# The last four gathers split into halves and the last norm rearranged, in a one-core streaming encoder step with expert retrieval

## The chip, the core and the metric

The kernel runs on one core of one Trainium2 chip. The metric is the device time of one execution in microseconds (us). The core has five engines that run their own instruction streams and wait for each other through semaphores: TensorE (PE, with its weight loads shown as PEld), VectorE (DVE), ScalarE (ACT), GpSimd (POOL) and SyncE (SP), and 16 DMA engines that serve the transfers issued by SP and POOL.

## What is computed

One inference step of a one-layer encoder for 384 tokens (256 of a new stream, 128 of running streams), in three tiles of 128 tokens. After attention and retention, each token goes through a layer that picks experts from a table of 16,384, and the result is normed. Only this last part is touched by the change:

```python
def rmsnorm(x, g):
    xf = x * lax.rsqrt(jnp.mean(x * x, axis=-1, keepdims=True) + EPS)
    return xf * g

def peer(h, ...):                       # 8 heads, 16 picks each: 128 picks a token
    ...                                 # e_idx: chosen experts, gate: softmax of their scores
    u = exp_u[e_idx]                    # (T, 8, 16, 1024)
    act = gelu(einsum('thkd,td->thk', u, h))
    return einsum('thk,thkd->td', gate * act, exp_v[e_idx])

x = x + peer(rmsnorm(x, ln2_g), ...)
y = rmsnorm(x, ln_final_g)
```

## The kernel before, in words

The expert tables U and V lie side by side in one HBM tensor `uv`: row `n` has the 1024 numbers of U and then the 1024 of V, 8 KB in fp32. The picks are worked off in 384 steps, n = 0 to 383: three tiles of tokens (t), eight heads in each, 16 picks a head. A head is a unit u (24 in all). A gather of step n fetches one row of 8 KB for each of the 128 partitions, 1 MB in all, into `row[n % 8]`, a ring of G = 8 buffers. A tile of 128 tokens is held twice over as two halves of 64, so an even n and the odd one after it form a pair: the even one serves 64 tokens with two picks and so does the odd one.

Each step has four stages.

- POOL (`gather`, L499) issues the gather of n once TensorE has done with the buffer: it waits for `acc`, which counts finished pairs. The gather's arrival raises `landed[s]`.
- DVE (L1879) waits for `landed[s]` and forms the dot product of the U half of the row with the token's normed vector.
- ACT (`weigh`, L1139) applies gelu, multiplies by the gate, and spreads the result into a diagonal matrix `diag[:, s, :]`: three instructions. The third raises `diagd`.
- PE (`add_experts`, L532) waits for both diagonals of the pair and multiplies them with the V halves, adding into two PSUM banks (e = 0 and e = 1, columns 0 to 511 and 512 to 1023 of the output). In the profile these are 8 records a pair. It then raises `acc`.

The order of everything that runs between these steps is written out by hand as generators, which a small clock advances once a step. In the last twenty-odd steps nothing else is left: the last unit's picks are spread in step 358 (`spread_take`, which fills `ids` and `gates`), and from there all engines only run the four stages.

Behind step 383 stands the last norm, of tile 2, in a straight line. ACT squares the two PSUM banks in one instruction of 128x1024 with a running sum (`square`), DVE turns the sum into a mean (`mean_square`, L1461), POOL raises it to the power -0.5 (`take_rstd`, L463), DVE multiplies PSUM by this factor and by the norm's weights `gfb` in two instructions of 128x512 (L1886), and SP stores each half as it is ready (L453). The program ends when both stores have landed.

```python
            mean_square(Y_STAT[2])
            dve.wait_ge(rsd, Y_STAT[2] + 1)
            dve.wait_ge(acc, UNITS * KP // 2)
            for e in range(2):
                then(V.scalar_tensor_tensor(x[:, 2, e * 512:(e + 1) * 512], ps[:, e, :], rstd[...], gfb[...], ALU.mult, ALU.mult), y_out)
```

`then` raises a semaphore with an instruction and makes DVE wait for it before the next.

Of the kernel before, what the change touches and what calls it, by code (L numbers as in the profile page):

```python
# [18 lines left out]
U32 = mybir.dt.uint32  # L19
ALU = mybir.AluOpType  # L20
# [3 lines left out]
P = 128  # L24
D = 1024
# [13 lines left out]
G = 8  # L39
# [43 lines left out]
def build(nc, a, o):  # L83
    with ExitStack() as ctx:
        def sb(name, shape, dt=F32):
            return ctx.enter_context(nc.sbuf_tensor(name, shape, dt))
# [16 lines left out]
        zdot = sb("zdot", [P, G])  # L103
        zact = sb("zact", [P, G])
        wgt = sb("wgt", [P, G])

        sumsq, ms, rstd = sb("sumsq", [P, 9]), sb("ms", [P, 9]), sb("rstd", [P, 9])
        bn6, mv = sb("bn6", [P, HB, 6]), sb("mv", [P, HB, 2])
# [165 lines left out]
        kv_out, sp_out, ss_out, y_done = sem("kv_out"), sem("sp_out"), sem("ss_out"), sem("y_done")  # L274
        sqd, msd, rsd, hready, x1_done = (sem(n) for n in ("squares", "mean_square", "rstd", "h_ready", "x1_done"))
        gained = sem("x_gained")
        ht_ps, ht_act, ht_dve = sem("ht_ps"), sem("ht_act"), sem("ht_dve")
        kv_ps, kv_sb, qi_ps, qi_sb, qa_ps, qa_sb = (sem(n) for n in ("kv_ps", "kv_sb", "qi_ps", "qi_sb", "qa_ps", "qa_sb"))
        vb_ps, vb_sb, qk_ps, rotated, gb_ps, gb_sb = (sem(n) for n in ("vb_ps", "vb_sb", "qk_ps", "rotated", "gb_ps", "gb_sb"))
# [81 lines left out]
        def _(sp):  # L361
# [87 lines left out]
            sp.wait_ge(y_out, 2)  # L449
            sp.dma_start(o["y"][1], x[:, 1, :]).then_inc(y_done, 16)  # L450
            for e in range(2):
                sp.wait_ge(y_out, 3 + e)
                sp.dma_start(o["y"][2][:, e * 512:(e + 1) * 512], x[:, 2, e * 512:(e + 1) * 512]).then_inc(y_done, 16)  # L453
            sp.wait_ge(sp_out, 16)
            sp.wait_ge(ss_out, 16)
# [2 lines left out]
        @block.gpsimd  # L458
        def _(pool):
            def take_rstd(n):  # L460

                pool.wait_ge(msd, n + 1)
                pool.tensor_tensor(rstd[:, n:n + 1], ms[:, n:n + 1], half4[:, 0:1], ALU.pow).then_inc(rsd, 1)  # L463

            def group_rstd(t):
                pool.wait_ge(o_var, t + 1)
                pool.tensor_tensor(rstd4[:], veps[:], half4[:], ALU.pow).then_inc(o_rstd, 1)

            pool.memset(euler[:], float(np.e))
            pool.memset(half4[:], -0.5).then_inc(half_set, 1)  # L470
            pool.wait_ge(half_set, 1)
            for n in range(TILES):
                take_rstd(n)
            pool.wait_ge(kv_ps, TILES)
            pool.memset(wz, 0.0).then_inc(wz_zero, 1)
            group_rstd(0)
            pool.wait_ge(wout, 2)
            pool.memset(wz, 0.0).then_inc(wz_zero, 1)
            take_rstd(H2_STAT[0])

            def gate_exp(u):

                pool.wait_ge(best_set, u + 1)
                pool.tensor_tensor(ebest[:, u % 2, :], euler[:, 0:1].broadcast_to([P, KP]), below[:], ALU.pow).then_inc(gexp, 1)  # L484

            gate_exp(0)
            gates_after = {gate_after(u): u for u in range(1, UNITS)}

            def gather(n):
                s = n % G  # L490
                if n % KP == 0:
                    pool.wait_ge(picked, n // KP + 1)
                if n == 4:
                    pool.wait_ge(qi_ps, 3)
                if n == 6:
                    pool.wait_ge(q_ps, 2)
                if n >= G:
                    pool.wait_ge(acc, (n - G) // 2 + 1)
                pool.indirect_dma_start(row[s], None, a["uv"], bass.IndirectOffsetOnAxis(  # L499
                    ap=ids[:, own(n // KP).start + n % KP:own(n // KP).start + n % KP + 1], axis=0)).then_inc(landed[s], 16)  # L500

            for n in range(UNITS * KP):
                gather(n)
                if n in gates_after:
                    gate_exp(gates_after[n])
                if n == 48:
                    group_rstd(1)
                if n == 50:
                    pool.wait_ge(o_ps, 2)
                    pool.memset(wz, 0.0).then_inc(wz_zero, 1)  # L510
                if n == 81:
                    take_rstd(H2_STAT[1])
                if n == 104:
                    pool.wait_ge(dots, CACHE + STREAMS)
                    pool.memset(qz, 0.0).then_inc(qz_zero, 1)
                if n == 124:
                    group_rstd(2)
                if n == 140:
                    take_rstd(Y_STAT[0])
                if n == 142:  # L520
                    pool.wait_ge(ss_ps, 1)
                    pool.memset(qzb, 0.0).then_inc(qzb_zero, 1)
                if n == 223:
                    take_rstd(H2_STAT[2])
                if n == 268:
                    take_rstd(Y_STAT[1])
            take_rstd(Y_STAT[2])

        @block.tensor
        def _(pe):  # L530
# [261 lines left out]
            def add_experts(n, stop=False):  # L792
                pe.wait_ge(diagd, n + 2)
                for e in range(2):
                    for j in range(2):
                        s = (n + j) % G
                        last = mm(ps[64 * j:64 * j + 64, Y_BANK[n // (HP * KP)] + e, :], diag[:, s, :], row[s][:, D + e * 512:D + (e + 1) * 512], False, stop)
                last.then_inc(acc, 1)

            mm(ps[:, 2, 0:P], e8[64:64 + HI, :], kiw[64:64 + HI, P:2 * P]).then_inc(w_ps, 1)  # L800
            index_queries(1, 6, 0, 1)
# [335 lines left out]
        def _(act):  # L1137
# [294 lines left out]
            for n in range(UNITS * KP):  # L1432
                t = n // (HP * KP)
                if n > 5:
                    weigh(n)
                if n == t * HP * KP + 1 and t > 0:
                    y_take(t - 1)
                clock.tick(n, *gens)
                if n == t * HP * KP + 3 and t > 0:
                    y_square(t - 1)  # L1440
            act.wait_ge(acc, UNITS * KP // 2)
            square(Y_STAT[2], psf[:, 0:D], h2r[0][:, 0, :])

        @block.vector
        def _(dve):
# [181 lines left out]
            def spread_take(u):  # L1627

                dve.wait_ge(spread_ps, u + 1)
                for q in range(2):  # L1630
                    r = slice(64 * q, 64 * q + 64)
                    src = spread_psum(u)[r, :].rearrange("p (j e c q) -> p e q c j", j=2, e=2, q=2)
                    V.tensor_copy(ids[r, own(u)].rearrange("p (c j) -> p c j", j=2), src[:, 0, q, :, :])
                    ins = V.tensor_copy(gates[r, own(u)].rearrange("p (c j) -> p c j", j=2), src[:, 1, q, :, :])
                then(ins, picked)

            def top16(u):
                yield from top16_halves(u)
# [233 lines left out]
            for n in range(UNITS * KP):  # L1872
# [6 lines left out]
                V.tensor_tensor_reduce(row[s][:, 0:D], row[s][:, 0:D], h2r[t % 2][:, n % 2, :], 1.0, 0.0, ALU.mult, ALU.add,  # L1879
                                       zdot[:, s:s + 1]).then_inc(dotted, 1)  # L1880
                clock.tick(n, *gens)
            mean_square(Y_STAT[2])
            dve.wait_ge(rsd, Y_STAT[2] + 1)
            dve.wait_ge(acc, UNITS * KP // 2)
            for e in range(2):
                then(V.scalar_tensor_tensor(x[:, 2, e * 512:(e + 1) * 512], ps[:, e, :], rstd[:, Y_STAT[2]:Y_STAT[2] + 1],  # L1886
                                            gfb[:, e * 512:(e + 1) * 512], ALU.mult, ALU.mult), y_out)


# ---- launch: inputs laid out for the program, outputs laid out as the reference has them  # L1890
# [56 lines left out]
```

## Time and profile before

| | |
|---|---|
| median of 3 runs | 1169.07 us (1169.01, 1169.07, 1171.17) |
| profiled execution, own time | 1169.1 us |
| its span, first to last instruction | 1167.3 us |
| mean granted TensorE clock | 0.892 of full speed |
| busy share of the span: PE, DVE, POOL, ACT | 74%, 70%, 46%, 38% |
| DMA | 461.82 MB, 396 GB/s over the span; 402.68 MB of it are the 384 gathers |

The span is 1.8 us shorter than the execution's own time; what lies around it is outside the instructions. A busy share is an average over the whole run, so the table says little about the end of the program, where the change lies. The page's row of DMA shows the 16 engines at 90% or more of their time in nearly every one of the 40 slices.

### The profile page before, as it was taken

The numbers are of one execution on the slowest core, as the hardware profiler recorded it, in microseconds if no ns is written. First come the engines' busy times: TensorE is split into PE (matmuls) and PEld (weight loads), VectorE is DVE, ScalarE is ACT, GpSimd is POOL, SyncE is SP. The second block draws the span as 40 slices with busy tenths as digits, with TensorE's granted clock in tenths as the row PEclk, the third lists the DMA queues.
The fourth block names the chain that finished last, engine by engine and source line by source line (L and its number), as shares of the span: only waits on it lengthen the run. The fifth ranks groups of instructions, "written<-read, shape, count | busy, mean of one in ns | idle before, by whom it ended". The sixth has DMA issues, their size and how long they took to land.

```text
span 1167.3 us, 12080 instructions
## 1 busy us (share of the span) xinstructions
PE 859.7 (74%) x3701; PEld 390.8 (33%) x3706; DVE 813.9 (70%) x2115; ACT 440.8 (38%) x1400; POOL 539.7 (46%) x431
## 2 busy tenths in 40 slices
PE   8999988998888757765767768577666656656554
PEld 6748644443323314322223333133222212211110
DVE  2426877875787789986877886547877777777453
ACT  2122444333444334433456553233333333333332
POOL 0002445552666455463644553445564555456441
PEclk9999999999999879787889999797989888886868
DMA  9903999999999999999999999999999999999994
GB/s 378 393 1 92 422 425 426 426 425 428 402 423 426 425 427 424 378 407 423 428 426 424 426 426 427 424 427 428 418 389 419 426 427 426 428 426 425 424 427 202
DMA packets 67057, 461.82 MB, mean 396 GB/s; under 512 B 8368, under 2 KB 10160, under 8 KB 15024
## 3 DMA queue, kind: packets, MB, share of 16 engines
q0 software_dynamic: 55296, 402.68, 82.5%
q1 hardware_dynamic: 11696, 58.37, 12.3%
q8 instruction: 29, 0.48, 0.1%
q14 instruction: 36, 0.29, 0.1%
HBM read 456.73 MB, written 3.24 MB: 394 GB/s over the span
## 4 chain that ended last, share of the span: by engine, by line
DMA 43%; PE 28%; DVE 15%; issue 6%; POOL 4%; ACT 3%; SPq 0%; DVEq 0%; POOLq 0%
DMA rows<-in_uv,ids 41%; PE ps L532 27%; DVE rows L1879 7%; POOL rows L499 4%; ACT work L1139 1%; DMA rows<-in_w_qi 1%; ACT wgt L1139 1%; DMA wt<-in_w_q 1%; POOL work L484 1%; ACT zact L1139 1%; DVE top L1476 1%; PE ps L535 1%; DVE wt L1480 1%; DVE work L1609 0%; DVE work L1613 0%
## 5 line engine op out<-in xcount | busy, mean ns | idle before, releaser
L499 POOL DMA_INDIRECT rows<-in_uv,ids x384 | 445.4, 1160 | 495.1 <-PE ps L532 428.1
L532 PE MATMUL ps<-rows,work 128*64 128x512 f32 x1536 | 458.8, 727 | 289.8 <-ACT work L1139 289.2
L1879 DVE CUSTOM_DVE_ANT_0 rows<-rows,masks 128x1024 f32<-128x1024 f32 x256 | 313.6, 1226 | 158.9 <-DMA rows<-in_uv,ids 153.0
L1139 ACT ACTIVATE zact<-zdot 128x1 f32<-128x1 f32 x384 | 77.6, 202 | 575.7 <-DVE zdot L1879 563.7
L532 PEld LDWEIGHTS ps<-rows,work 128*64 128x64 f32 x1536 | 106.4, 155 | 549.2 <-ACT work L1139 389.6
L1879 DVE CUSTOM_DVE_ANT_0 rows<-rows,wt 128x1024 f32<-128x1024 f32 x128 | 156.9, 1226 | 85.9 <-DMA rows<-in_uv,ids 80.7
L532 PE MATMUL ps<-wt 128*128 128x128 f32 (+7 forms) x599 | 155.7, 414 | 0.9 <-DVE wt L1655 0.9
L1139 ACT ACTIVATE work<-pair,wgt 128x64 f32<-128x64 f32 x384 | 133.5, 348 | 12.5
L1139 ACT ACTIVATE wgt<-zact,gates 128x1 f32<-128x1 f32 x384 | 113.1, 294 | 12.5
L532 PEld LDWEIGHTS ps<-work,wt 128*128 128x128 f32 (+1 forms) x712 | 90.1, 201 | 60.5 <-issue 60.5
L532 PEld LDWEIGHTS ps<-wt 128*128 128x128 f32 (+2 forms) x604 | 89.2, 192 | 55.3 <-issue 47.1
L532 PE MATMUL ps<-work,wt 128*128 128x128 f32 (+1 forms) x712 | 103.9, 294 | 4.8 <-DMA wt<-in_w_q 4.8
L484 POOL TENSOR_TENSOR work<-euler,below 128x16 f32<-128x16 f32 x24 | 77.9, 3245 | 21.8 <-DVE below L1593 20.4
L1139 ACT ACTIVATE wt<-ps 128x512 f32<-128x512 f32 (+5 forms) x61 | 34.7, 577 | 58.0 <-PE ps L532 44.7
L1139 ACT ACT_TABLE_LOAD x25 | 32.1, 1283 | 1.2 <-PEq L1930 0.7
L1879 DVE DVE_READ_ACCUMULATOR2_ANT zdot<- 128x1 f32 x384 | 31.5, 82 | 0.0
L532 PE MATMUL ps<-wt,work 128*128 128x512 f32 x64 | 29.3, 600 | 0.0
L1139 ACT ACTIVATE work<-ps 128x256 f32<-128x256 f32 (+2 forms) x49 | 16.8, 345 | 29.2 <-PE ps L535 14.8
L463 POOL TENSOR_TENSOR rstd<-ms,half 128x1 f32<-128x1 f32 x9 | 6.8, 760 | 38.3 <-DVE ms L1461 38.2
L532 PE MATMUL ps<-wt,rows 128*128 128x128 f32 x192 | 22.9, 276 | 1.0 <-DMA rows<-in_w_qi 1.0
L532 PEld LDWEIGHTS ps<-wt,rows 128*128 128x128 f32 x192 | 22.1, 192 | 1.7 <-DMA rows<-in_w_qi 1.5
L532 PEld LDWEIGHTS ps<-keysT,work 128*128 128x128 f32 x96 | 14.1, 210 | 24.2 <-issue 24.1
(145 smaller groups left out, 639.0 us busy)
## 6 DMA issues: line engine op xcount, KB each, us to landing
wt<-in_w_q SPq DMA_DIRECT2D x9, 2048.0 KB, 15.9
rows<-in_uv,ids POOLq DMA_INDIRECT x384
rows<-in_w_out SPq DMA_DIRECT2D x2, 2048.0 KB, 32.0
wt<-in_w_out SPq DMA_DIRECT2D x2, 2048.0 KB, 11.3
wt<-in_ckv SPq DMA_DIRECT2D x16, 256.0 KB, 14.0
x<-in_x SPq DMA_DIRECT2D x5, 512.0 KB, 8.5
rows<-in_w_qi SPq DMA_DIRECT2D x1, 2048.0 KB, 12.8
wt<-in_w_qa SPq DMA_DIRECT2D x1, 2048.0 KB, 11.6
```

The source lines that it names most:

```text
L463: pool.tensor_tensor(rstd[:, n:n + 1], ms[:, n:n + 1], half4[:, 0:1], ALU.pow).then_inc(rsd, 1)
L484: pool.tensor_tensor(ebest[:, u % 2, :], euler[:, 0:1].broadcast_to([P, KP]), below[:], ALU.pow).then_inc(gexp, 1)
L499: pool.indirect_dma_start(row[s], None, a["uv"], bass.IndirectOffsetOnAxis(ap=ids[:, own(n // KP).start + n % KP:own(n // KP).start + n % ...
L532: return nc.tensor.matmul(out, lhsT, rhs, start=start, stop=stop)
L535: return nc.tensor.transpose(out, in_, ident[0:k, 0:k])
L1139: return nc.scalar.activation(*args, **kw)
L1476: then(V.max(out=top8[:], in_=score))
L1480: then(V.match_replace(out=score, in_to_replace=top8[:], in_values=score, imm_value=TAKEN))
L1879: V.tensor_tensor_reduce(row[s][:, 0:D], row[s][:, 0:D], h2r[t % 2][:, n % 2, :], 1.0, 0.0, ALU.mult, ALU.add, zdot[:, s:s + 1]).then_inc( ...
```

## The change

The last four steps, 380 to 383, no longer fetch whole rows. `gather_last` first issues the four U halves (each 128 x 4 KB, into the same buffers, each raising `landed[s]` as before), then the V halves of 380, 381 and 382 (each with a semaphore of its own, `v_landed[0..2]`), and at last the V half of 383 as two quarters (128 x 2 KB, `v_landed[3]` and `v_landed[4]`). The row numbers for this are made from `ids` by two shifts on DVE behind the last `spread_take`, which raise `last_set`. TensorE waits for the V halves in `add_experts`, and raises `y_half` after the e = 0 matmuls of the last pair. Behind pair 378/379 it gets 9 more matmuls of 128x512 in bf16, and behind pair 380/381 two, whose results nobody reads.

The last norm is divided by column halves: ACT squares bank 0 at `y_half` and bank 1 at `acc`; DVE multiplies each bank by `gfb` into `x` ahead of the factor; the sum of both halves and EPS is one DVE instruction (the division by 1024 went into the squares' scale). When the factor is there, DVE scales columns 0 to 511 and ACT columns 512 to 1023. SP stores the first half on `y_out` and the second on `y_last`.

```diff
+            def gather_last():
+                first = UNITS * KP - 4
+                pool.wait_ge(last_set, 1)
...
+                for j in range(4):
+                    pool.wait_ge(acc, (first + j - G) // 2 + 1)
+                    s = (first + j) % G
+                    pool.indirect_dma_start(row[s][:, 0:D], None, halves, half[j]).then_inc(landed[s], 16)
+                for j in range(3):
+                    s = (first + j) % G
+                    pool.indirect_dma_start(row[s][:, D:2 * D], None, halves, half[j], element_offset=D).then_inc(v_landed[j], 16)
+                for e in range(2):
+                    s = (first + 3) % G
+                    pool.indirect_dma_start(row[s][:, D + e * 512:D + (e + 1) * 512], None, quarters, quarter,
+                                            element_offset=D + e * 512).then_inc(v_landed[3 + e], 16)
...
             def add_experts(n, stop=False):
                 pe.wait_ge(diagd, n + 2)
                 for e in range(2):
+                    if n == UNITS * KP - 4 and e == 0:
+                        pe.wait_ge(v_landed[0], 16)
+                        pe.wait_ge(v_landed[1], 16)
+                    if n == UNITS * KP - 2:
+                        if e == 0:
+                            pe.wait_ge(v_landed[2], 16)
+                        else:
+                            last.then_inc(y_half, 1)
+                        pe.wait_ge(v_landed[3 + e], 16)
...
                 last.then_inc(acc, 1)
+                if n in (UNITS * KP - 6, UNITS * KP - 4):
+                    for i in range(9 if n == UNITS * KP - 6 else 2):
+                        mm(ps[:, 6, :], ident_bf[:], ident_bf[:].rearrange("p (g t) -> p g t", g=1).broadcast_to([P, 4, P]))
...
+            act.wait_ge(y_half, 1)
+            A(h2r[0][:, 1, 0:512], ps[:, 0, :], ACT.Square, scale=D ** -0.5, accum_out=sumsq[:, 0:1]).then_inc(half_sqd, 1)
             act.wait_ge(acc, UNITS * KP // 2)
-            square(Y_STAT[2], psf[:, 0:D], h2r[0][:, 0, :])
+            A(h2r[0][:, 1, 512:D], ps[:, 1, :], ACT.Square, scale=D ** -0.5,
+              accum_out=sumsq[:, Y_STAT[2]:Y_STAT[2] + 1]).then_inc(sqd, 1)
+            act.wait_ge(rsd, Y_STAT[2] + 1)
+            act.wait_ge(gained, 4)
+            A(x[:, 2, 512:D], x[:, 2, 512:D], ACT.Copy, scale=rstd[:, Y_STAT[2]:Y_STAT[2] + 1]).then_inc(y_last, 1)
...
+                if u == UNITS - 1:
+                    four = ids[:, own(u).start + KP - 4:own(u).start + KP]
+                    V.tensor_scalar(last_ids[:, 0:4], four, 1, None, ALU.logical_shift_left)
+                    then(V.tensor_scalar(last_ids[:, 4:5], four[:, 3:4], 2, None, ALU.logical_shift_left), last_set)
...
-            mean_square(Y_STAT[2])
+            dve.wait_ge(half_sqd, 1)
+            then(V.tensor_tensor(x[:, 2, 0:512], ps[:, 0, :], gfb[:, 0:512], ALU.mult), gained)
+            dve.wait_ge(sqd, Y_STAT[2] + 1)
+            then(V.tensor_scalar(ms[:, Y_STAT[2]:Y_STAT[2] + 1], sumsq[:, 0:1], sumsq[:, Y_STAT[2]:Y_STAT[2] + 1], EPS,
+                                 ALU.add, ALU.add), msd)
+            then(V.tensor_tensor(x[:, 2, 512:D], ps[:, 1, :], gfb[:, 512:D], ALU.mult), gained)
             dve.wait_ge(rsd, Y_STAT[2] + 1)
-            dve.wait_ge(acc, UNITS * KP // 2)
-            for e in range(2):
-                then(V.scalar_tensor_tensor(x[:, 2, e * 512:(e + 1) * 512], ps[:, e, :], rstd[:, Y_STAT[2]:Y_STAT[2] + 1],
-                                            gfb[:, e * 512:(e + 1) * 512], ALU.mult, ALU.mult), y_out)
+            then(V.tensor_scalar(x[:, 2, 0:512], x[:, 2, 0:512], rstd[:, Y_STAT[2]:Y_STAT[2] + 1], None, ALU.mult), y_out)
```

What this does to the order of instructions shows at three places. The first is the end of GpSimd's row: before the change, the last unit's 16 gathers and the power (L463).

```order
L499 DMA rows<-in_uv,ids 128x2048 [waits acc] x15
L499 DMA rows<-in_uv,ids 128x2048 [waits acc,picked]
L499 DMA rows<-in_uv,ids 128x2048 [waits acc] x15
L463 TENSOR_TENSOR rstd<-ms,half 128x1 [waits mean_square]
L84 UNCONDITIONAL_BRANCH
```


After the change the last unit has 12 whole gathers, and the last four steps have nine pieces.

```order
L506 DMA rows<-in_uv,ids 128x2048 [waits acc,picked]
L506 DMA rows<-in_uv,ids 128x2048 [waits acc] x11
L520 DMA rows<-in_uv,last_ids 128x1024 [waits acc,last_set]
L520 DMA rows<-in_uv,last_ids 128x1024 [waits acc] x3
L523 DMA rows<-in_uv,last_ids 128x1024 x3
L526 DMA rows<-in_uv,last_ids 128x512 x2
L470 TENSOR_TENSOR rstd<-ms,half 128x1 [waits mean_square]
```


Four issues became nine, and the power (now L470) stands behind all of them.

The second place is the end of TensorE's row. Before the change the last two pairs read like all the others (`rows` are the gathered rows, `work` the diagonals):

```order
L532 MATMUL ps<-rows,work 64x512 [waits diagd]
L532 MATMUL ps<-rows,work 64x512 x3
L532 MATMUL ps<-rows,work 64x512 [waits diagd]
L532 MATMUL ps<-rows,work 64x512 x3
L84 UNCONDITIONAL_BRANCH
```


After the change, from pair 378/379 on:

```order
L562 MATMUL ps<-rows,work 64x512 [waits diagd]
L562 MATMUL ps<-rows,work 64x512 x3
L562 MATMUL ps<-ident_bf 128x512 x9
L562 MATMUL ps<-rows,work 64x512 [waits v_landed1,v_landed0,diagd]
L562 MATMUL ps<-rows,work 64x512 x3
L562 MATMUL ps<-ident_bf 128x512 x2
L562 MATMUL ps<-rows,work 64x512 [waits v_landed3,v_landed2,diagd]
L562 MATMUL ps<-rows,work 64x512
L562 MATMUL ps<-rows,work 64x512 [waits v_landed4]
L562 MATMUL ps<-rows,work 64x512
```


The added bf16 matmuls stand ahead of the waits for the V halves, and the last pair is cut in two by the wait for `v_landed4`.

The third place is the end of VectorE's row. Before the change (`keep` holds the norm's weights):

```order
L1879 ISA rows,zdot<-rows,masks 128x1024 [waits landed7]
L1879 ISA zdot 128x1
L1461 TENSOR_SCALAR ms<-sumsq 128x1 [waits squares]
L1886 SCALAR_TENSOR_TENSOR x<-ps,rstd,keep 128x512 [waits acc,rstd,mean_square]
L1886 SCALAR_TENSOR_TENSOR x<-ps,rstd,keep 128x512 [waits y_out]
L84 UNCONDITIONAL_BRANCH [waits y_out]
```


After the change:

```order
L1931 ISA rows,zdot<-rows,masks 128x1024 [waits landed7]
L1931 ISA zdot 128x1
L1935 TENSOR_TENSOR x<-ps,keep 128x512 [waits half_sqd]
L1937 TENSOR_SCALAR ms<-sumsq 128x1 [waits squares,x_gained]
L1939 TENSOR_TENSOR x<-ps,keep 128x512 [waits mean_square]
L1941 TENSOR_SCALAR x<-x,rstd 128x512 [waits rstd,x_gained]
L84 UNCONDITIONAL_BRANCH [waits y_out]
```


The two multiplications by the weights moved ahead of the wait for `rstd`, and one multiplication by `rstd` stays behind it; the other is ACT's.

## Rows read from the trace of the kernel before

**Rows 1.** The page of the profile: span, chain by engine, one costly group

```profile
span 1167.3 us, 12080 instructions
...
DMA 43%; PE 28%; DVE 15%; issue 6%; POOL 4%; ACT 3%; SPq 0%; DVEq 0%; POOLq 0%
...
L499 POOL DMA_INDIRECT rows<-in_uv,ids x384 | 445.4, 1160 | 495.1 <-PE ps L532 428.1
...
L1879 DVE DVE_READ_ACCUMULATOR2_ANT zdot<- 128x1 f32 x384 | 31.5, 82 | 0.0
```

**Rows 2.** Timeline of all engines from 1145 us: start, duration, engine, operation, idle before

```profile
1145.60 1.23 DVE L1879 CUSTOM_DVE_ANT_0 rows<-rows,masks 128x1024 f32<-128x1024 f32 x1 [1.25 <-DMA rows<-in_uv,ids]
...
1152.93 1.23 DVE L1879 CUSTOM_DVE_ANT_0 rows<-rows,masks 128x1024 f32<-128x1024 f32 x1 [1.22 <-DMA rows<-in_uv,ids]
...
1155.38 1.23 DVE L1879 CUSTOM_DVE_ANT_0 rows<-rows,masks 128x1024 f32<-128x1024 f32 x1 [1.21 <-DMA rows<-in_uv,ids]
...
1157.61 1.94 PE L532 MATMUL ps<-rows,work 128*64 128x512 f32 x8 [1.49 <-ACT work L1139]
...
1159.60 1.02 ACT L1139 ACTIVATE masks<-ps 128x1024 f32<-128x1024 f32 x1 [2.04 <-PE ps L532]
...
1160.74 0.15 DVE L1461 TENSOR_SCALAR ms<-sumsq 128x1 f32<-128x1 f32 x1 [4.13 <-ACT masks L1139]
1160.98 0.57 POOL L463 TENSOR_TENSOR rstd<-ms,half 128x1 f32<-128x1 f32 x1 [18.25 <-DVE ms L1461]
1161.66 1.54 DVE L1886 SCALAR_TENSOR_TENSOR x<-ps,rstd,keep 128x512 f32<-128x512 f32 x2 [0.76 <-POOL rstd L463]
1162.44 1.12 SPq L453 DMA_DIRECT2D out_y<-x  x2
```

**Rows 3.** Stretches: length, busy us of PE, PEld, DVE, ACT, POOL, PEclk, DMA share, GB/s

```profile
1105.00:1145.00 40.00, 22.26 (x62) 5.16 (x64) 19.73 (x32) 13.54 (x49) 19.52 (x16) 0.72 1.01 425
1151.00:1155.00 4.00, 2.29 (x6) 0.68 (x8) 1.95 (x4) 1.58 (x6) 0.00 (x0) 0.75 0.07 29
1163.20:1164.90 1.70, 0.00 (x0) 0.00 (x0) 0.00 (x0) 0.00 (x0) 0.00 (x0) 0.52 0.82 308
```

**Rows 4.** Timeline of GpSimd, the first and last of its last four gathers

```profile
1136.73 1.10 POOL L499 DMA_INDIRECT rows<-in_uv,ids  x1 [2.57 <-PE ps L532]
...
1141.49 1.24 POOL L499 DMA_INDIRECT rows<-in_uv,ids  x1 [0.30 <-issue]
```

**Rows 5.** DMA queues from 540 to 600 us: packets, MB, share of 16 engines

```profile
q0 software_dynamic: 3307, 24.09, 95.2%
q1 hardware_dynamic: 537, 1.44, 6.0%
```

**Rows 6.** Timeline of TensorE, four bursts: start, duration, idle before

```profile
1118.45 3.68 PE L532 MATMUL ps<-rows,work 128*64 128x512 f32 x8 [1.17 <-ACT work L1139]
...
1142.92 3.55 PE L532 MATMUL ps<-rows,work 128*64 128x512 f32 x8 [2.96 <-ACT work L1139]
1147.83 1.94 PE L532 MATMUL ps<-rows,work 128*64 128x512 f32 x8 [1.37 <-ACT work L1139]
1152.71 3.41 PE L532 MATMUL ps<-rows,work 128*64 128x512 f32 x8 [2.94 <-ACT work L1139]
```

**Rows 7.** Stretches, TensorE alone: length, PE busy, PEclk, DMA share, GB/s

```profile
6.00:8.00 2.00, 2.00 (x10) 1.00 1.05 429
1147.20:1152.60 5.40, 1.94 (x8) 1.00 0.63 267
```

**Rows 8.** Groups of instructions by line and shape: count, busy us, mean ns

```profile
L1699 DVE TENSOR_TENSOR work<-x,keep 128x512 f32<-128x512 f32 x2 | 1.4, 693 | 0.1
...
L1604 DVE TENSOR_SCALAR work<-work 128x16 uint32<-128x16 uint32 x24 | 4.3, 179 | 0.2
...
L1703 DVE TENSOR_SCALAR work<-work,rstd 128x1024 f32<-128x1024 f32 x1 | 0.8, 753 | 0.7 <-POOL rstd L463 0.7
...
L1139 ACT ACTIVATE wt<-ps 128x512 f32<-128x512 f32 x36 | 21.0, 590 | 36.7 <-PE ps L532 24.9 <-PE ps L535 11.8
```

More of the change, by code:

```diff
@@ L105, in build @@
         wgt = sb("wgt", [P, G])
+        last_ids = sb("last_ids", [P, 5], U32)
         sumsq, ms, rstd = sb("sumsq", [P, 9]), sb("ms", [P, 9]), sb("rstd", [P, 9])
@@ L276, in build @@
         gained = sem("x_gained")
+        v_landed = [sem(f"v_landed{i}") for i in range(5)]
+        last_set = sem("last_set")
+        y_half, y_last, half_sqd = sem("y_half"), sem("y_last"), sem("half_sqd")
         ht_ps, ht_act, ht_dve = sem("ht_ps"), sem("ht_act"), sem("ht_dve")
@@ L451, in _ @@
             for e in range(2):
-                sp.wait_ge(y_out, 3 + e)
+                if e == 0:
+                    sp.wait_ge(y_out, 3)
+                else:
+                    sp.wait_ge(y_last, 1)
                 sp.dma_start(o["y"][2][:, e * 512:(e + 1) * 512], x[:, 2, e * 512:(e + 1) * 512]).then_inc(y_done, 16)
@@ L500, in gather @@
                     ap=ids[:, own(n // KP).start + n % KP:own(n // KP).start + n % KP + 1], axis=0)).then_inc(landed[s], 16)
+            def gather_last():
+                first = UNITS * KP - 4
+                pool.wait_ge(last_set, 1)
+                half = [bass.IndirectOffsetOnAxis(ap=last_ids[:, j:j + 1], axis=0) for j in range(4)]
+                quarter = bass.IndirectOffsetOnAxis(ap=last_ids[:, 4:5], axis=0)
+                halves = a["uv"].rearrange("n (i d) -> (n i) d", i=2)
+                quarters = a["uv"].rearrange("n (i d) -> (n i) d", i=4)
+                for j in range(4):
[9 more added lines that the diff above has]
+                                            element_offset=D + e * 512).then_inc(v_landed[3 + e], 16)
             for n in range(UNITS * KP):
-                gather(n)
+                if n < UNITS * KP - 4:
+                    gather(n)
+                elif n == UNITS * KP - 4:
+                    gather_last()
                 if n in gates_after:
@@ L794, in add_experts @@
                 for e in range(2):
+                    if n == UNITS * KP - 4 and e == 0:
+                        pe.wait_ge(v_landed[0], 16)
+                        pe.wait_ge(v_landed[1], 16)
+                    if n == UNITS * KP - 2:
+                        if e == 0:
+                            pe.wait_ge(v_landed[2], 16)
+                        else:
+                            last.then_inc(y_half, 1)
+                        pe.wait_ge(v_landed[3 + e], 16)
                     for j in range(2):
```

## Prediction

> **What bounds the kernel now.** I start with the page. Its chain of waits gives DMA the largest share, 43% of the span, and the 384 gathers are issued by one line [rows 1]. Then the timeline of the last 25 us: VectorE's dots of steps 379, 382 and 383 start at 1145.60, 1152.93 and 1155.38, each after 1.2 us of idle time that a gather ended [rows 2]. So gathers land every (1155.38 - 1145.60) / 4 = 2.445 us, and arrivals alone set the pace. From 1105 to 1145 the DMA engines have a share of 1.01 and move 425 GB/s; from 1151 to 1155, when two gathers have yet to land, the share is 0.07, about one engine of 16 [rows 3]. One engine is late, and it alone decides when the last two gathers count as landed. Whatever is changed here is worth what it does to this engine's last work and to the straight line behind it.
>
> That line, from the last landing at 1155.38 to the end [rows 2]: dot and three ScalarE instructions, 2.23 us, until TensorE starts at 1157.61; the last pair, 1.94, to 1159.55; squares, from 1159.60 until VectorE's mean starts at 1160.74; the power and the wait for it, 0.92, until 1161.66; the first store is issued at 1162.44. The span ends at 1167.3, 4.86 us after that issue. Of these, 1163.2 to 1164.9 is the time in which both stores' bytes move (0.82 of 1.70 us) [rows 3]. They follow each other without a hole, since each half takes about as long as the 0.75 us between the issues. So the first issue, not the second, sets the end: end = first issue + 4.86.
>
> **The change, part by part.**
>
> *The pieces.* The same 4 MB are fetched in nine pieces instead of four. The late engine works off its queue in order: U halves of 380 to 383, V halves of 380 to 382, two quarters. If bytes alone counted, the second V half (step 381) would land when the third whole gather did, at 1152.93, and the last quarter at 1155.38. The price of a piece is not in the trace, since no gather is that small. The nearest rows are the two queues between 540 and 600 us [rows 5]. Over 960 us of 16 engines, the gathers' queue has 3307 packets of 7.28 KB on average at 0.276 us each, the other queue 537 of 2.68 KB at 0.107 us. A straight line through both gives 0.0088 us a packet whatever its size. A piece more is 8 more data packets an engine and one that signals the end: 9 x 0.0088 = 0.08 us. Up to the second V half there are six pieces in place of three gathers, +0.24 us: it lands at 1153.17. The last quarter has five more pieces behind it: 1155.38 + 0.40 = 1155.78. Bounds: nothing, and 0.5 us a piece (below).
>
> Here a rule of the Trainium skill speaks against the change. Its page "DMA: Bandwidth & Descriptors", section "Anatomy of one DMA — SWDGE (gpsimd) path", puts a fixed 2.0 us on each DMA, plus bytes over 436 GB/s; as an estimate by that, 1 MB takes 4.4 us, and three pieces more would delay the second V half by 6 us. The trace has a gather landing every 2.445 us, so with a queue of several the fixed part is hidden; the sum above goes by the trace.
>
> *GpSimd.* The whole gathers 380 to 383 were issued from 1136.73 to 1142.73, the last two after a wait for buffers [rows 4]. The four U issues take these places. Five more follow; at 0.30 us between issues [rows 4] and 1.16 us each [rows 1] they end at 1142.73 + 5 x 1.46 = 1150.0. The late engine comes to the last quarter only at about 1155.1, so the issues are 5 us ahead of it. The 15 engines that are not late run out at about 1150.5 before and may now wait for POOL, which costs nothing, because the late one sets the landing. The power behind the issues is wanted at 1158.
>
> *Dots and diagonals.* The U half of 383 lands five pieces before the end, three halves and two quarters, or about 5 us: near 1150.7. VectorE needs 1.23 us a dot [rows 2] plus 0.08 for reading the sum [rows 1], a little more than a half's 1.22 us, so its dot of 383 ends by about 1152.2, and the diagonal is there about 1 us later, 1153.2. It is hidden behind the V halves; before, this 2.23 us lay on the path.
>
> *The bf16 matmuls.* Nine go behind pair 378/379, which runs 1147.83 to 1149.77 at the full clock [rows 6, 7]. Between 6 and 8 us of the run such matmuls took about 0.2 us each at the upper level of 2.4 GHz (10 records in 2 us) [rows 7], so nine end at 1151.6, 1.5 us before the V half of 381. They are hidden. The two behind pair 380/381 are not: 0.4 us on the path.
>
> *TensorE.* Starting at 1153.2: pair 380/381 takes 1.94, the two others 0.4, the last pair 1.94. Its e = 0 half starts at about 1155.55 and its e = 1 half at 1156.5, and both quarters have landed by then (1155.1 and 1155.78). End: 1153.2 + 4.3 = 1157.5 instead of 1159.55. **Gain 2.05 us**, if TensorE is at 2.4 GHz. Between 1147.2 and 1152.6 the granted clock is 1.00 [rows 7]; it fell, after a pause of 2.94 us, when TensorE began again at 1152.71, and that pair took 3.41 us [rows 6], with 0.75 as the clock of 1151 to 1155 [rows 3]. With the nine matmuls the pause shrinks to about 1.5 us, so I take the upper level for both pairs.
>
> *The norm.* The second square is 128x512. ScalarE has 590 ns for a pass over a PSUM bank of that size [rows 8] against 1.02 us for both banks [rows 2]: 0.43 less, so the mean starts 1160.74 - 1159.55 - 0.43 = 0.76 us after TensorE. The first half's square and product with the weights start 0.97 us before TensorE's end and are done by then. Behind the mean, the product of bank 1 ends after 0.15 + 0.09 + 0.69 [rows 2, 8] = 0.93, as long as the power and its wait (0.92) [rows 2], so the scaling starts 0.97 after the mean; 128x1024 took 753 ns [rows 8], so half of it, with its fixed part, 0.46. First store issued 0.76 + 0.97 + 0.46 + 0.02 = 2.21 us after TensorE's end, against 1162.44 - 1159.55 = 2.89. **Gain 0.68.** Bounds: 0.4 (scaling without its faster form) and 0.9. ScalarE's half is ready at about the time at which SP has done with the first issue, so the stores' 1.5 us of bytes still lie back to back.
>
> *The shifts.* Two instructions of 0.18 us [rows 8] and one wait, in step 358, under VectorE's 1.2 us of idle time a step [rows 2]. Nothing; without that cover 0.4 us.
>
> **Sum.** 2.05 + 0.68 = 2.7 us off the profiled execution's 1169.1, which is the median of 1169.07 within noise: 1166.4 us. A measurement of this kernel tells about 0.2% (2.3 us) from no change, so the forecast is just beyond it, at 0.23%.
>
> **The rivals.**
>
> *A. The forecast*, 1166.4 (1166.0 to 1167.0 by the prices of pieces and norm): 0.67.
>
> *B. TensorE is at 1.2 GHz when the nine matmuls start.* The bursts before alternate between 1.94 us and 3.4 to 3.7 [rows 6], so another execution can have the slow one at 1147.83. The pair then ends at 1151.4, and nine matmuls at twice 0.2 us hold TensorE until 1155.0 unless the clock rises among them. That is 1.8 us behind the V half. What follows is fast, since TensorE has been busy all along: gain 2.7 - 1.8 = 0.9, 1168.2. For it: the pair at 1118.45 was slow throughout though one ran shortly before. Against it: of the last four bursts two were fast, at 1147.83 and 1157.61 [rows 2, 6], and a rise early among the nine leaves the forecast intact. 0.17.
>
> *C. The price of a piece is larger.* At 0.5 us, half of what GpSimd takes to issue one, three pieces cost 1.5 us to the second V half, and 1167.6 comes out. For it: no row shows a gather of 4 KB rows. Against it: 2.7 KB packets ran at 95% of the gathers' rate per byte [rows 5]. 0.07. From 0.9 us a piece the gain is gone.
>
> *D. Slower: the clock stays at 1.2 GHz from pair 378/379 to the end.* The nine end at 1155.0, the two pairs take 3.6 each and the two others 0.8: 1163.0 against 1159.55, 3.45 later, less 0.68: +2.8, 1171.9. It decides when the low level lasts through pair 380/381 as well: from then on the loss exceeds 1 us. Against it: the low bursts ended with the clock back up, as the fast pair at 1147.83 after the slow one at 1142.92 [rows 6]. 0.06.
>
> *E. Slower: a fixed cost of each piece is not hidden*, as the page's rule would have it. From issue to end the last stores need 4.86 us, of which about 1.5 are bytes: at most 3.3 us of fixed time. Were it paid on each of three more pieces, the second V half would be 10 us later and the time 1176. Against it: the rows' 2.445 us a gather. 0.03.
>
> **How the numbers follow.** Faster by over 0.2% (below 1166.7): most of A, 0.53. Within 0.2%: the rest of A, B and C, 0.38. Slower: D and E, 0.09. The range takes in A, B and C and leaves D and E out: 1165.8 (pieces free, best norm) to 1168.6.
>
> **What would show it.** Right: dots of the last four steps 1.3 us apart, diagonals done before the V halves land, both last pairs at 1.94 us with a clock of 1.00, TensorE's end about 2.1 us before the place that it had relative to the step 379 landing, 2.2 us from there to the first store. Wrong: landings of the halves more than 1.3 us apart (C, E); the nine matmuls in 3.8 us and pair 380/381 starting as they end (B); pairs of 3.5 us (D).

## The result: 15 us slower, in a place that the change does not name

The changed kernel takes 1184.81 us (median of 4 runs, 1183.86 to 1185.35) against 1169.04 before: a ratio of 1.0126, 95% interval 1.0113 to 1.0139. Forecast were 1166.4 us and a range up to 1168.6.

The page of the changed kernel shows the same bytes, moved more slowly:

```profile
span 1182.0 us, 12118 instructions
...
q0 software_dynamic: 55888, 402.68, 82.9%
...
DMA 47%; PE 26%; DVE 14%; POOL 4%; issue 4%; ACT 3%; SPq 0%; DVEq 0%; ACTq 0%; POOLq 0%
```

The span grew by 14.7 us. The gathers' queue has 592 packets more than the 55296 of before and the same 402.68 MB (seven halves for four gathers at 144 packets each are 432 more, and 160 are left for the two quarters: 80 each, or 5 an engine, where the prediction counted 9); the chain's share of DMA rose from 43% to 47% [rows 1]. The stretch of 1105 to 1145 us (columns as in [rows 3]), and below it one of 600 to 700 us, where no changed operation runs at all:

```profile
600.00:700.00 100.00, 71.81 (x342) 34.69 (x344) 75.27 (x196) 57.05 (x150) 52.49 (x38) 0.90 1.01 418
1105.00:1145.00 40.00, 21.76 (x66) 4.95 (x64) 19.68 (x37) 13.52 (x48) 15.92 (x16) 0.80 1.01 419
```

425 GB/s [rows 3] became 419, and from 600 to 700 us 426 in the kernel before became 418, both at a share of 1.01. The DMA engines are as busy as before, and get less done. The timeline of VectorE's last dots shows it gather by gather (columns as in [rows 2]):

```profile
1134.62 1.23 DVE L1931 CUSTOM_DVE_ANT_0 rows<-rows,masks 128x1024 f32<-128x1024 f32 x1 [1.21 <-DMA rows<-in_uv,ids]
...
1159.58 1.22 DVE L1931 CUSTOM_DVE_ANT_0 rows<-rows,masks 128x1024 f32<-128x1024 f32 x1 [1.27 <-DMA rows<-in_uv,ids]
...
1162.07 1.23 DVE L1931 CUSTOM_DVE_ANT_0 rows<-rows,masks 128x1024 f32<-128x1024 f32 x1 [1.26 <-DMA rows<-in_uv,ids]
...
1163.34 1.23 DVE L1931 CUSTOM_DVE_ANT_0 rows<-rows,masks 128x1024 f32<-128x1024 f32 x1
...
1167.16 1.23 DVE L1931 CUSTOM_DVE_ANT_0 rows<-rows,masks 128x1024 f32<-128x1024 f32 x1
```

From 1134.62 to 1162.07 are eleven whole gathers at 2.495 us each; before it was 2.445 [rows 2]. The dot of step 379 starts 16.5 us later than before (1162.07 against 1145.60), and all of that was lost ahead of the first piece. What comes behind it, up to the first store, took less time than before, by nearly what was forecast. The rest of the same timeline:

```profile
1164.30 3.29 PE L562 MATMUL ps<-rows,work 128*64 128x512 f32 x8 [3.06 <-ACT work L1181]
...
1167.52 2.41 PE L562 MATMUL ps<-ident_bf 128*128 128x512 bf16 x9
...
1169.86 1.94 PE L562 MATMUL ps<-rows,work 128*64 128x512 f32 x8
...
1171.73 0.60 PE L562 MATMUL ps<-ident_bf 128*128 128x512 bf16 x2
...
1172.27 1.94 PE L562 MATMUL ps<-rows,work 128*64 128x512 f32 x8
...
1175.04 0.21 DVE L1937 TENSOR_SCALAR ms<-sumsq 128x1 f32<-128x1 f32 x1 [0.24 <-ACT masks L1181]
...
1175.34 0.57 POOL L470 TENSOR_TENSOR rstd<-ms,half 128x1 f32<-128x1 f32 x1 [8.68 <-DVE ms L1937]
1176.02 0.48 DVE L1941 TENSOR_SCALAR x<-x,rstd 128x512 f32<-128x512 f32 x1
...
1176.53 0.82 SPq L460 DMA_DIRECT2D out_y<-x  x2
```

From the dot of 379 to TensorE's end: 1174.21 - 1162.07 = 12.14 us, before 1159.55 - 1145.60 = 13.95. From there to the first store 2.32, before 2.89. Only what comes behind the store grew, from 4.86 to 1182.0 - 1176.53 = 5.47. The tail gained 1.8 us in all. This execution also meets the condition of the forecast's rival B: pair 378/379 runs slowly, in 3.29 us, and pair 380/381 starts as the nine bf16 matmuls end. B's price is not there, though. The nine took 2.41 us and not 3.8, since the granted clock rose among them (the number ahead of the DMA share, columns as in [rows 3]):

```profile
1167.00:1168.00 1.00, 1.00 (x4) 0.21 (x3) 0.95 (x3) 0.79 (x3) 0.00 (x0) 0.50 1.01 406
1168.00:1169.00 1.00, 1.00 (x6) 0.46 (x5) 0.40 (x2) 0.56 (x4) 0.00 (x0) 0.92 0.99 401
1169.00:1170.00 1.00, 1.00 (x7) 0.34 (x7) 0.00 (x0) 0.34 (x1) 0.00 (x0) 1.00 0.57 229
```

They end at about 1169.9, and the V half of 381 can be expected at 1169.8 (an estimate: 1162.07 and the 7.59 us that e1 below has from the dot of 379 to pair 380/381, with three gathers' bytes at 0.05 us more each). So the slow pair cost about 0.1 us, not 1.8.

### The profile page after: what moved, and what is told of

Its sections match the earlier page's. It is cut to its first block, busy times and chain, and to the rows that moved or that the text cites. A ratio compares the mean times of both kernels' runs of the same rounds, so it can differ in the third digit from the quotient of the medians.

```text
span 1182.0 us, 12118 instructions
## 1 busy us (share of the span) xinstructions
PE 871.4 (74%) x3712; PEld 392.6 (33%) x3717; DVE 814.3 (69%) x2118; ACT 441.5 (37%) x1403; POOL 537.0 (45%) x436
## 3 DMA queue, kind: packets, MB, share of 16 engines
q0 software_dynamic: 55888, 402.68, 82.9%
## 4 chain that ended last, share of the span: by engine, by line
DMA 47%; PE 26%; DVE 14%; POOL 4%; issue 4%; ACT 3%; SPq 0%; DVEq 0%; ACTq 0%; POOLq 0%
DMA rows<-in_uv,ids 45%; PE ps L562 26%; DVE rows L1931 7%; POOL rows L506 3%; ACT work L1181 1%; DMA rows<-in_w_qi 1%; DMA wt<-in_w_q 1%; ACT wgt L1181 1%; POOL work L491 1%; ACT zact L1181 1%; DVE top L1524 1%; DVE wt L1528 1%; PE ps L565 1%; DVE work L1661 0%; DVE work L1657 0%
## 5 line engine op out<-in xcount | busy, mean ns | idle before, releaser
L562 PE MATMUL ps<-rows,work 128*64 128x512 f32 x1536 | 470.2, 743 | 289.4 <-ACT work L1181 289.1
L506 POOL DMA_INDIRECT rows<-in_uv,ids x380 | 431.5, 1136 | 513.3 <-PE ps L562 448.6
L474 POOL TENSOR_TENSOR rstd<-veps,half 128x4 f32<-128x4 f32 x3 | 4.2, 1385 | 36.4 <-DVE veps L1578 36.4
L1524 DVE MAX8 top<-wt 128x8 f32<-128x640 f32 (+2 forms) x33 | 19.9, 602 | 1.1
```

The lines of the kernel that those rows point to most:

```text
L562: return nc.tensor.matmul(out, lhsT, rhs, start=start, stop=stop)
L1524: then(V.max(out=top8[:], in_=score))
```

## The cause, and the experiments

What can slow all gathers by 2% and has no operation of its own? The changed kernel declares a small buffer, `last_ids`, ahead of `rows`. This is where the compiled programs put the buffers, in bytes from the start of a partition:

```
                 rows            wt              masks
before           32512 = 127*256  98048 = 383*256  196352 = 767*256
changed          32544 (+32)      98080            196384
```

The 20 bytes of `last_ids` take 32, and everything behind it starts 32 bytes later. **Theory 1**: a packet of a gather is dearer when it is written to an address that is no multiple of some power of two. **Theory 2**, the main rival: something else in the change, the nine semaphores, the shifts, the longer programs. A third, that the engines read the shifted buffers more slowly, has something against it from the start: the dots take 1.23 us as before and fast pairs 1.94 us.

### e1: last_ids behind all buffers

```diff
-        last_ids = sb("last_ids", [P, 5], U32)
         sumsq, ms, rstd = sb("sumsq", [P, 9]), ...
...
         keep = sb("keep", [P, 2048])
+        last_ids = sb("last_ids", [P, 5], U32)
```

> The changed kernel, with last_ids allocated behind all other buffers, so that rows starts at byte 32512 of a partition again (a multiple of 256, as before the change) and not at 32544. In the trace of the changed kernel the dots of whole gathers are 2.495 us apart instead of 2.445, long before step 380. Theory 1 (start address of the buffers behind last_ids): the spacing goes back to 2.445, which gives back 383 x 0.05 = 19 us of the 384 gathers less what other stages hide, and the time is that of before less the tail's own gain (1.2 to 2.7 us): 1166 to 1168. Theory 2 (something else that the change adds, its nine semaphores, the shifts, the longer programs, or the pieces): the spacing stays at 2.49 and the time at 1184 to 1185.

Measured: 1167.09 us against 1170.49 for the kernel before on the same chip, ratio 0.9977 (0.9967 to 0.9986). All that the change adds is still there, and the loss is gone: theory 2 falls. The timeline of e1 has the gathers at the old spacing (1138.15, 1140.59, 1143.05), and the end reads like the prediction's sum:

```profile
1138.15 1.22 DVE L1931 CUSTOM_DVE_ANT_0 rows<-rows,masks 128x1024 f32<-128x1024 f32 x1 [1.21 <-DMA rows<-in_uv,ids]
...
1140.59 1.23 DVE L1931 CUSTOM_DVE_ANT_0 rows<-rows,masks 128x1024 f32<-128x1024 f32 x1 [1.21 <-DMA rows<-in_uv,ids]
...
1143.05 1.22 DVE L1931 CUSTOM_DVE_ANT_0 rows<-rows,masks 128x1024 f32<-128x1024 f32 x1 [1.22 <-DMA rows<-in_uv,ids]
...
1147.74 1.94 PE L562 MATMUL ps<-rows,work 128*64 128x512 f32 x8 [1.32 <-ACT work L1181]
...
1149.61 2.12 PE L562 MATMUL ps<-ident_bf 128*128 128x512 bf16 x9
...
1153.10 1.94 PE L562 MATMUL ps<-rows,work 128*64 128x512 f32 x8 [1.37 <-DMA rows<-in_uv,last_ids]
...
1154.97 0.60 PE L562 MATMUL ps<-ident_bf 128*128 128x512 bf16 x2
...
1155.50 1.94 PE L562 MATMUL ps<-rows,work 128*64 128x512 f32 x8
...
1158.28 0.21 DVE L1937 TENSOR_SCALAR ms<-sumsq 128x1 f32<-128x1 f32 x1 [0.24 <-ACT masks L1181]
...
1158.58 0.57 POOL L470 TENSOR_TENSOR rstd<-ms,half 128x1 f32<-128x1 f32 x1 [9.65 <-DVE ms L1937]
1159.26 0.48 DVE L1941 TENSOR_SCALAR x<-x,rstd 128x512 f32<-128x512 f32 x1
...
1159.77 0.82 SPq L460 DMA_DIRECT2D out_y<-x  x2
```

### e2, e3, e4: the kernel before, shifted

e2 puts 32 unused bytes ahead of `rows`, e3 the same 32 between `rows` and `wt`, e4 64 bytes ahead of `rows`. Nothing else is changed.

```diff
+        pad = sb("pad", [P, 8])        # e2; [P, 16] in e4
         rows = sb("rows", [P, G, 2 * D])
```

> The kernel before, with an unused buffer of 32 bytes a partition ahead of rows: rows and all behind it start 32 bytes later, nothing else differs. Theory 1 (start address): whole gathers 2.495 us apart, time 1185 to 1187, the changed kernel's 1184.8 plus the gain of its tail. Theory 2 (anything else in the change): 1169.

> The kernel before, with the 32 unused bytes between rows and wt: rows starts at 32512 as before, while wt, masks, work and keep are shifted by 32 bytes. If it is the place where gathers are written that counts: spacing 2.445 and a time of 1169 to 1170 (the weight loads into wt may lose a little). If it is the place from which the engines read work, masks or wt: up to 1185.

> The kernel before, with 64 unused bytes ahead of rows: rows starts at 32576, a multiple of 64 but not of 128 or 256. The Trainium skill's page DMA: Bandwidth & Descriptors, section How a descriptor splits into AXI transactions, speaks of pieces that start at multiples of 256 B; by that rule this is as slow as 32 bytes, about 1185. If only multiples of 64 count, 1169.

| | rows starts at | time (us) | ratio to before, interval |
|---|---|---|---|
| e2 | 32544, 32 past a multiple of 256 | 1186.97 | 1.0150 (1.0137 to 1.0163) |
| e3 | 32512; wt and the rest shifted by 32 | 1171.95 | 1.0012 (1.0002 to 1.0023) |
| e4 | 32576, 64 past | 1183.72 | 1.0117 (1.0103 to 1.0132) |

An unused buffer of 32 bytes costs the old kernel 16.5 us. It is the ring into which the gathers write: shifting only what lies behind it leaves the dots 2.445 us apart, and the time grows by about 1.4 us (0.2 to 2.7), barely clear of nothing. What that is made of is not shown: in e3's profiled execution, with a span 2.4 us longer than that of before, the last dot starts 0.8 us later (1156.17 against 1155.38), and the last pair took 3.62 us instead of 1.94, at the lower clock, which e6 below met as well (3.68) at a median like that of before. The last dots in e2, 2.49 us apart and of the old length:

```profile
1167.02 1.23 DVE L1880 CUSTOM_DVE_ANT_0 rows<-rows,masks 128x1024 f32<-128x1024 f32 x1 [1.26 <-DMA rows<-in_uv,ids]
...
1169.51 1.23 DVE L1880 CUSTOM_DVE_ANT_0 rows<-rows,masks 128x1024 f32<-128x1024 f32 x1 [1.26 <-DMA rows<-in_uv,ids]
...
1172.00 1.23 DVE L1880 CUSTOM_DVE_ANT_0 rows<-rows,masks 128x1024 f32<-128x1024 f32 x1 [1.26 <-DMA rows<-in_uv,ids]
```

And the gathers' queue on its page:

```profile
q0 software_dynamic: 55296, 402.68, 82.5%
```

82.5% of a longer span (1185.1 us) for the 55296 packets of before (82.5% of 1167.3, from the page of before): 1185.1 x 16 x 0.825 / 55296 = 0.2829 us a packet against 0.2787, 4.2 ns more. Nine packets an engine and gather make 0.04 us, most of the 0.048 between 2.493 and 2.445 us (mean distance of the last 19 dots in e2 and in the kernel before).

### e5, e6: where the limit lies

The same kernel with `ids` (128 bytes) moved behind `keep`, and with `ids` and `gates` (256 bytes), so that all buffers start earlier.

```diff
-        ids = sb("ids", [P, RING * KP], U32)
-        gates = sb("gates", [P, RING * KP])        # e6 only
...
         keep = sb("keep", [P, 2048])
+        ids = sb("ids", [P, RING * KP], U32)
+        gates = sb("gates", [P, RING * KP])        # e6 only
```

> The kernel before, with the 128 bytes of ids allocated behind keep: rows starts at 32384, a multiple of 128 and not of 256. 32 bytes off gave 2.491 us a gather and 1187.0 us, 64 off 2.482 and 1183.7, no shift 2.444 and 1170.5. Theory 1a (each packet that starts off a multiple of 256 B is dearer): 2.46 to 2.49 and 1177 to 1184. Theory 1b (multiples of 128 are enough): 2.444 and 1170.

> The kernel before, with the 256 bytes of ids and gates allocated behind keep: rows starts at 32256, which is another address than before but again a multiple of 256. Theory 1 (the remainder of the address by 256 counts): 2.444 us a gather, 1170. Rival (it is the absolute place, or any move of the buffers against each other): 2.48 to 2.49 us and over 1180.

e5: 1183.31 us, ratio 1.0110 (1.0089 to 1.0131), 2.482 us a gather. e6: 1169.89 us, ratio 0.9995 (0.9984 to 1.0005), 2.445. So neither the place nor the move counts, but the remainder by 256, as far as the five places tried tell: 128 past a multiple costs almost as much as 64 or 32, and 256 nothing. The stretch of 1105 to 1145 us in e5, then in e6:

```profile
1105.00:1145.00 40.00, 22.82 (x66) 5.20 (x66) 20.19 (x35) 13.00 (x46) 17.17 (x17) 0.79 1.01 418
```

```profile
1105.00:1145.00 40.00, 24.56 (x67) 5.24 (x66) 19.74 (x32) 13.56 (x49) 18.92 (x16) 0.67 1.01 427
```

The Trainium skill has a rule of this kind, on the page "DMA: Bandwidth & Descriptors", section "How a descriptor splits into AXI transactions": a piece of a transfer is cut into transactions of 256 B, each of which must start at a multiple of 256 B, and where the piece does not, the first one starts at the multiple below it and the bytes before the piece are fetched for nothing. It speaks of addresses read. The runs show a price of the same multiple where SBUF is written; that the same splitting is the reason is not shown. That 128 past a multiple still costs agrees with it. That 32 past, where by the rule the fewest bytes would be wasted, is the dearest (ratio 1.0150 against 1.0117 and 1.0110, 3 to 4 us) is not explained by it and stays open.

### e7, e8, e9: the parts of the tail

With the address out of the way, each part of the change can be weighed. e7 is e1 without the eleven bf16 matmuls, e8 is e1 with the old norm, e9 is the kernel before with the new norm alone.

```diff
-                if n in (UNITS * KP - 6, UNITS * KP - 4):         # e7
-                    for i in range(9 if n == UNITS * KP - 6 else 2):
-                        mm(ps[:, 6, :], ident_bf[:], ...)
```

```diff
-            act.wait_ge(y_half, 1)                                # e8; e9 adds the - lines to the kernel before
-            A(h2r[0][:, 1, 0:512], ps[:, 0, :], ACT.Square, ...)
...
+            square(Y_STAT[2], psf[:, 0:D], h2r[0][:, 0, :])
```

> The changed kernel with last_ids behind all buffers (1167.1 us) without the eleven bf16 matmuls. In the run with them both last pairs took 1.94 us at a clock of 1.00. If they keep the clock up: pair 380/381 takes 3.4 to 3.6 us, and TensorE ends 1.3 to 3 us later, less the 0.5 us of the two that stand between the pairs: 1168 to 1169.5. If they do nothing: 0.5 us less, 1166.6.

> The changed kernel with last_ids behind all buffers (1167.1 us) with the last norm of before: the pieces and the bf16 matmuls alone. In that kernel's trace the new norm issues the first store 2.33 us after TensorE's end instead of 2.89 us (0.56 gained), but the span ends 5.53 us after this issue instead of 4.86 (0.67 lost), the second issue being 0.4 us behind the first instead of 0.78. If the second store's own issue has nothing to do with it: this kernel is 0.6 us slower, 1167.7, with 5.5 us behind the first issue. If two issues close together cost what the norm gains: 4.86 us behind the first issue and the same time, 1167.1.

> The kernel before with the new last norm alone: whole gathers, no bf16 matmuls, no last_ids, rows at 32512. By the traces of e1 and e8 the norm issues the first store 0.55 us earlier after TensorE's end. If the norm's rearrangement also lengthens what follows the issue (5.5 us against 4.86 in the kernels with the old norm and whole gathers), the span gains nothing and the time is that of before, 1170.2 to 1170.5. If the longer end in e1 and e8 comes from the pieces, 0.5 us less: 1169.7.

| | time (us) | ratio to before, interval |
|---|---|---|
| e1, whole change | 1167.09 | 0.9977 (0.9967 to 0.9986) |
| e7, no bf16 matmuls | 1168.60 | 0.9990 (0.9978 to 1.0002) |
| e8, old norm | 1168.10 | 0.9976 (0.9963 to 0.9989) |
| e9, new norm alone | 1170.90 | 1.0009 (0.9999 to 1.0019) |

*The bf16 matmuls* are worth about 1.5 us in the medians of e1 and e7, but their intervals overlap. TensorE in e7's profiled execution:

```profile
1146.70 1.94 PE L562 MATMUL ps<-rows,work 128*64 128x512 f32 x8 [1.46 <-ACT work L1178]
...
1152.05 5.17 PE L562 MATMUL ps<-rows,work 128*64 128x512 f32 x16 [3.41 <-DMA rows<-in_uv,last_ids]
```

After a pause of 3.41 us both last pairs take 5.17 us together; with the eleven matmuls, in e1, it was 4.34 from 1153.10 to 1157.44, the two others in it. That is 0.8 us. The granted clock in e7 was 0.50 from 1152 to 1155 us, in the first of the two pairs, and 1.00 at the end; pair 378/379 ahead of the pause had been fast.

The kernels without these matmuls meet the same in their last pair: it took 1.94 us in the profiled executions of the kernel before, e4 and e9, and 2.91 to 3.68 in those of e2, e3, e5 and e6. With the nine matmuls both last pairs were fast in all five profiled executions (1.94 each in the changed kernel, e1, e8 and e11, 3.83 together in e10). So the execution of before on which the prediction rests had the shorter of the two ends, and against one of the others the matmuls would be worth more; how often each occurs was not counted.

*The norm* gains nothing that can be measured: e8 has the ratio of e1 (its median is 1.0 us higher, well inside the intervals), and e9 that of no change. Yet in every trace it does what was forecast up to the store: 2.32 to 2.33 us after TensorE's end instead of 2.88 to 2.89. What is lost lies behind the store. The last issues and the span of three traces show it; first e8 (old norm), with its page's span:

```profile
1160.66 1.12 SPq L457 DMA_DIRECT2D out_y<-x  x2
```

```profile
span 1165.9 us, 12117 instructions
```

then e9 (new norm, whole gathers):

```profile
1162.20 0.82 SPq L457 DMA_DIRECT2D out_y<-x  x2
```

```profile
span 1167.3 us, 12091 instructions
```

From the first issue to the end of the span: 4.86 us in the kernel before (4.8 to 4.9 in e2 to e6 as well), 5.24 in e8, 5.10 in e9, 5.53 in e1. The bytes of both stores have moved 2.3 to 2.4 us after the first issue in those of before, e1, e8 and e9, so what differs is what follows the last byte. Both parts of the change have a share in it: the pieces and the bf16 matmuls with the old norm add 0.4 us (e8), the new norm with whole gathers 0.2 (e9), one execution each.

### e10, e11: fewer bf16 matmuls, one store

e10 is e1 with the nine matmuls and without the two; e11 is e1 with one store of 128x1024 instead of two of 128x512.

```diff
-                if n in (UNITS * KP - 6, UNITS * KP - 4):         # e10
-                    for i in range(9 if n == UNITS * KP - 6 else 2):
+                if n == UNITS * KP - 6:
+                    for i in range(9):
```

```diff
-            for e in range(2):                                    # e11
-                if e == 0:
-                    sp.wait_ge(y_out, 3)
-                else:
-                    sp.wait_ge(y_last, 1)
-                sp.dma_start(o["y"][2][:, e * 512:(e + 1) * 512], x[:, 2, e * 512:(e + 1) * 512]).then_inc(y_done, 16)
+            sp.wait_ge(y_out, 3)
+            sp.wait_ge(y_last, 1)
+            sp.dma_start(o["y"][2], x[:, 2, :]).then_inc(y_done, 16)
```

> e1 (the change with last_ids behind all buffers, 1167.1 us) without the two bf16 matmuls between the last two pairs; the nine stay. They take 0.53 us in e1's trace (1154.97 to 1155.50 until the last pair starts). If the clock stays up without them: 0.5 us less, 1166.6, with both pairs at 1.94 us. If it falls: the last pair takes up to 3.5 us, 1168.5.

> e1 with one store of 128x1024 after both halves are scaled, instead of two stores. It is issued when ScalarE is done, 0.26 us after the first store's issue in e1. If two issues within 0.4 us are what makes the end 5.5 us long: at most 4.9 us behind the issue, and 0.3 us less than e1. If the end has a length of its own: 5.5 us behind it and 0.3 us more than e1, 1167.4.

e10: 1167.35 us, ratio 0.9983 (0.9974 to 0.9992); e11: 1167.56, ratio 0.9980 (0.9971 to 0.9989). Neither is told from e1. In e10's trace TensorE does what was hoped for:

```profile
1151.28 2.12 PE L562 MATMUL ps<-ident_bf 128*128 128x512 bf16 x9
...
1154.75 3.83 PE L562 MATMUL ps<-rows,work 128*64 128x512 f32 x16 [1.35 <-DMA rows<-in_uv,last_ids]
```

Both pairs in 3.83 us instead of 4.34, but half a microsecond is less than these runs can resolve (the interval reaches 1.1 us to either side). In e11 the span ends 5.16 us behind its one issue (1160.84 to 1166.0); that is 0.37 us less than in e1, and still not 4.86, so two issues close together are at most a part of it. The issue itself comes 0.34 us later behind TensorE's end than in e1, which takes the 0.37 back. Why the end takes 4.8 to 5.5 us stays open. e1 beats the kernel before by 0.2% (interval 0.1 to 0.3%) and the changed kernel by far, and no other version here is measurably better.

## Why the prediction was wrong

**The step that failed** is the first one of "The pieces": "If bytes alone counted, the second V half (step 381) would land when the third whole gather did, at 1152.93". It takes the time of before for everything ahead of step 380, and the sum, "2.05 + 0.68 = 2.7 us off the profiled execution's 1169.1", has no term for the line `last_ids = sb("last_ids", [P, 5], U32)`, though the diff has it. That line shifted the ring by 32 bytes and put 0.05 us on each whole gather, 16.5 us by step 379. e1 and e2 show it from both sides: the change without the shift gains, the shift without the change loses. No rival had it. D and E, which took the slower side, put the loss in the last four steps, and neither occurred.

**The pieces and TensorE (2.05 us): right.** In e1 pair 380/381 starts at 1153.10 when its V half lands (forecast 1153.17), the last pair ends at 1157.44 (forecast 1157.5). The price of 0.08 us a piece from the line through two queues held: the dot of step 379 starts at 1145.51, and 1153.10 is 7.59 us behind it, where three whole gathers took 7.33 before; that is 0.26 for three pieces, forecast 0.24. Only the two quarters were mis-counted, with 5 packets an engine and not 9, and they never set the pace. The fixed 2.0 us that the Trainium skill puts on each DMA (page "DMA: Bandwidth & Descriptors", section "Anatomy of one DMA — SWDGE (gpsimd) path") was rightly left out of the sum for a queue of several: three pieces cost 0.26 us here, not 6.

**The diagonals: right.** The dots of the U halves follow each other at VectorE's own rate (1163.34 to 1167.16, 1.27 us apart in the changed kernel; 1.25 in e1) and the last one ends at 1151.8 in e1, before its V halves are there.

**The bf16 matmuls: right in kind.** In e1 the nine end at about 1151.7 and the next pair is fast. Rival B's condition, a slow pair 378/379, is real, as the changed kernel's own execution shows, but its 1.8 us are not: the clock rose among the nine, the exception that B itself named, and the loss was about 0.1 us.

**The norm (0.68 us): half right.** From TensorE's end to the first store it took 2.33, forecast 2.21, before 2.89: a gain of 0.56. The rule "end = first issue + 4.86" failed: it was 5.1 to 5.5 in the kernels with the new norm and 5.24 with the pieces and the old norm (e8), so the 0.56 did not reach the end, and in e9 the norm alone gains nothing (ratio 1.0009, 0.9999 to 1.0019).

**The size of the tail.** e1's ratio of 0.9977 is 2.7 us at 1170, what the sum gave, but that they agree this well is luck. The interval reaches from 1.6 to 3.9 us, and the profiled executions of e1 and of the kernel before differ by 2.0: 2.11 at TensorE's end, 0.56 more at the first store, 0.67 less behind it. The pieces with the bf16 matmuls carry the gain (e8), not the norm. A part of it may be that they also spare TensorE the slow last pair, which the sum did not count because its execution had none; this was not tested by itself.

## What to carry to other kernels

Before costing what a diff computes, look at what it declares: a buffer of 20 bytes ahead of the big ones moved them all by 32, and a kernel that is bound by gathers lost 1.3% over its whole length. Put small new buffers behind the large ones that gathers write, or check that these still start at a multiple of 256 bytes. When a change of the last 20 us moves the time by 15, compare a stretch in which nothing was changed first: the GB/s from 600 to 700 us told it at once.

## What the runs showed of the hardware

The price of a gather into SBUF depends on where the buffer starts, by 256 bytes: 2.445 us for 1 MB at a multiple (two addresses: the kernel before and e6), 2.493 at 32 past (e2), 2.484 at 64 past (e4), 2.482 at 128 past (e5), each in rows of 8 KB and as the mean of the last 18 distances. With `wt` and the buffers behind it shifted by 32 bytes, and the ring left alone, the kernel took about 1.4 us more (e3, interval of the ratio 1.0002 to 1.0023), for a reason that no run isolates. VectorE's dots took no longer in a shifted buffer: 1.225 us in e2 against 1.226.

The DMA share stayed at 1.01 while the rate fell from 426 to 418 GB/s: a full share says that the engines are busy, not that they move what they could.
